# Ends of four program blocks, and the turning of an expert's 16 context rows, in a hybrid diffusion layer

## The reference, cut to what matters

```python
def _expert_choice_ffn(h, p):
    B, N, D = h.shape
    cap = EC_FACTOR * N // N_EXPERTS            # 256 latent rows, 16 context rows
    probs = jax.nn.softmax((h @ p['w_router']).astype(jnp.float32), axis=-1)
    gates, idx = lax.top_k(jnp.swapaxes(probs, 1, 2), cap)
    xsel = jax.vmap(lambda hb, ib: hb[ib])(h, idx)
    hid = jax.nn.silu(jnp.einsum('becd,edf->becf', xsel, p['w_gate'])) * jnp.einsum('becd,edf->becf', xsel, p['w_up'])
    yo = jnp.einsum('becf,efd->becd', hid, p['w_down']) * gates[..., None].astype(h.dtype)
    return jax.vmap(lambda ib, yb: jnp.zeros((N, D), yb.dtype).at[ib.reshape(-1)].add(yb.reshape(-1, D)))(idx, yo)

def _layer(x, cvec, p, states, grid):
    mods = (jax.nn.silu(cvec) @ p['w_ada'] + p['b_ada'])[..., None, :]
    sh1, sc1, g1, sh2, sc2, g2 = jnp.split(mods, 6, axis=-1)
    h = _rmsnorm(x, p['norm1_g']) * (1 + sc1) + sh1
    o, new_states = _mixers(h, p, states, grid)     # h @ w_in, three mixers, @ w_out
    x = x + g1 * o
    h = _rmsnorm(x, p['norm2_g']) * (1 + sc2) + sh2
    return x + g2 * _expert_choice_ffn(h, p), new_states
```

## Time and profile before

| | us |
|---|---|
| runs | 3442.53, 3443.15, 3450.62 |
| median | 3443.15 |
| profiled execution | 3448.97 |
| its span | 3447.2 |
| PE busy in the span | 3111.8 (90%) |
| VectorE, ScalarE, GpSimd busy | 2279.6, 1609.5, 878.8 |

### The profile page before, as it was taken

One profiled execution on the slowest core, in us unless ns is written; L12 is line 12 of the kernel. 1 busy time (PEld: TensorE's weight loads), 2 busy tenths in 40 slices (PEclk: granted clock), 3 DMA queues, 4 the chain that ended last, 5 costly groups with the idle time before them and its releaser, 6 DMA issues. The chain is left out here.

```text
span 3447.2 us, 90906 instructions
## 1 busy us (share of the span) xinstructions
PE 3111.8 (90%) x37105; PEld 2856.9 (83%) x37105; DVE 2279.6 (66%) x4490; ACT 1609.5 (47%) x2917; POOL 878.8 (25%) x1232
## 2 busy tenths in 40 slices
PE   7899989999689999999869961999999999999996
PEld 4887867767489999999857740999999999999996
DVE  5565549995478888888777758555555555555555
ACT  3313656665445545554456530444444444444454
POOL 0110000000066667676422201012111111111113
PEclk8999989999899999999989975999999999999998
DMA  6455336665644554444276632556656556556685
GB/s 203 139 163 170 94 88 203 201 198 152 186 122 108 131 151 111 110 109 109 56 209 186 177 125 76 165 186 196 208 186 195 186 185 194 185 184 190 206 286 187
DMA packets 583428, 561.43 MB, mean 163 GB/s; under 512 B 211550, under 2 KB 527262, under 8 KB 582138
## 3 DMA queue, kind: packets, MB, share of 16 engines
q1 hardware_dynamic: 546652, 446.02, 43.2%
q0 software_dynamic: 36016, 109.52, 10.8%
q10 hardware_dynamic: 432, 1.25, 0.1%
HBM read 418.33 MB, written 138.33 MB: 161 GB/s over the span
## 5 line engine op out<-in xcount | busy, mean ns | idle before, releaser
L3456 DVE TENSOR_TENSOR exp_wlo<-exp_raw,exp_whi 128x2048 fp32r<-128x2048 f32 x192 | 439.9, 2292 | 366.3 <-ACT exp_whi L3357 354.4
L3357 ACT CAST exp_whi<-exp_raw 128x2048 fp32r<-128x2048 f32 x189 | 360.0, 1905 | 76.8 <-DMA exp_raw<-in_w_up 74.2
L1042 PE MATMUL mix_acc<-proj_hThi,mix_wlo 128*128 128x448 f32 (+3 forms) x920 | 357.6, 389 | 14.4 <-DVE mix_wlo L1410 14.4
L1042 PE MATMUL mix_acc<-proj_hTlo,mix_whi 128*128 128x448 f32 (+3 forms) x920 | 335.6, 365 | 0.0
L1042 PE MATMUL mix_acc<-proj_hThi,mix_whi 128*128 128x448 f32 (+3 forms) x920 | 335.4, 365 | 0.0
L3286 PE MATMUL moe_o<-moe_hidhi,exp_wlo 128*128 128x272 f32 x1024 | 307.5, 300 | 2.6 <-DVE moe_hidlo L3570 2.6
L3286 PE MATMUL moe_g<-moe_xThi,exp_wlo 128*128 128x272 f32 x1024 | 300.1, 293 | 1.0 <-DVE moe_xTlo L3460 1.0
L3286 PE MATMUL moe_o<-moe_hidhi,exp_whi 128*128 128x272 f32 x1024 | 297.8, 291 | 0.0
L3286 PE MATMUL moe_g<-moe_xThi,exp_whi 128*128 128x272 f32 x1024 | 297.3, 290 | 0.0
L3286 PE MATMUL moe_u<-moe_xThi,exp_wlo 128*128 128x272 f32 x1024 | 296.7, 290 | 0.0
L3286 PE MATMUL moe_u<-moe_xThi,exp_whi 128*128 128x272 f32 x1024 | 296.4, 289 | 0.0
(11 more groups left out here) (395 smaller groups left out, 8539.5 us busy)
## 6 DMA issues: line engine op xcount, KB each, us to landing
exp_raw<-in_w_gate SPq DMA_DIRECT2D x64, 1024.0 KB, 5.0
exp_raw<-in_w_up SPq DMA_DIRECT2D x64, 1024.0 KB, 5.1
exp_raw<-in_w_down SPq DMA_DIRECT2D x64, 1024.0 KB, 6.7
scn_plain<-rec SPq DMA_DIRECT2D x68, 384.0 KB, 3.8
rec<-mix_arena SPq DMA_DIRECT2D x24, 896.0 KB, 4.4
proj<-mix_out POOLq DMA_DIRECT2D x88, 224.0 KB, 2.5
scn_grc<-grec SPq DMA_DIRECT2D x136, 128.0 KB, 3.9
mix_arena<-in_w_ada SPq DMA_DIRECT2D x12, 1024.0 KB, 5.8
```

The lines of the kernel that those rows point to most:

```text
L1042: mm = pe.matmul(acc[n % ACCS][0:width, 0:tn], wt[:, k, 0:width], hT[hp][:, k, t0:t0 + tn], start=k == 0 and i == 0, stop=k == KD - 1 and ...
L3357: act.copy(w[k % RING][0][:, :, :], raw[k % RAW][:, :, :]).then_inc(hi_done[k % RING], 1)
L3456: dve.tensor_tensor(w[k % RING][1][:, :, :], raw[k % RAW][:, :, :], w[k % RING][0][:, :, :], ALU.subtract).then_inc(lo_done[k % RING], 1)
```

## The change

Five edits. (a) Norm: GpSimd's wait for its stores is made by SP. (b) Mix: the last four of the 115 unit stores are issued by SP, in its slots ahead of the GLA record of that slot, with semaphores of their own; GpSimd's final waits are SP's. (c) Route: GpSimd has no list any more; the four picks stand first in the experts block. (d) Experts: the waits for the last scatters and stores are SP's. (e) `turn`: the third transposition takes 16 rows by 128 columns, with a 16 by 16 identity, and writes 16 columns.

```diff
@@ project_norm
+                for u in range(2):
+                    sp.wait_ge(v_stored[u], 32 * (9 - u))
...
-                for u in range(2):
-                    pool.wait_ge(v_stored[u], 32 * (9 - u))
@@ project_and_prepare
+    LAST_UNITS = UNITS - 4
...
+                def store_unit(n):
+                    c0, width = MIX_COLS[n // NB]
+                    t0, tn = MIX_BLOCKS[n % NB]
+                    sp.wait_ge(evacuated, n + 1)
+                    sp.dma_start(proj[c0:c0 + width, t0:t0 + tn], out[n % OUTS][0:width, 0:tn]).then_inc(last_stored[n % OUTS], 16)
+
                 for n in range(SLOTS):
+                    if LAST_UNITS < n <= UNITS:
+                        store_unit(n - 1)
...
                 sp.wait_ge(qk_stored, 16 * 4)
+                for u in range(OUTS):
+                    sp.wait_ge(out_stored[u], 16 * ((LAST_UNITS - 1 - u) // OUTS + 1))
+                    sp.wait_ge(last_stored[u], 16 * 2)
...
-                for n in range(SLOTS):
-                    if 1 <= n <= UNITS:
-                        store(n - 1)
-                for u in range(OUTS):
-                    pool.wait_ge(out_stored[u], 16 * ((UNITS - 1 - u) // OUTS + 1))
+                for n in range(LAST_UNITS):
+                    store(n)
...
-                    if n >= OUTS:
+                    if n >= LAST_UNITS + OUTS:
+                        act.wait_ge(last_stored[n % OUTS], 16)
+                    elif n >= OUTS:
                         act.wait_ge(out_stored[n % OUTS], 16 * (n // OUTS))
@@ stage_route
-            @block.gpsimd
-            def _(pool):
-                pool.wait_ge(out_done, 6)
-                pool.wait_ge(picked_out, 16)
-                for e in range(2):
-                    pick(pool, parts, picked, e)
+                sp.wait_ge(picked_out, 16)
@@ stage_experts
+                for u in range(HELD):
+                    sp.wait_ge(f_stored[u], 16 * held(u))
+                sp.wait_ge(late1_out, 48)
+                sp.wait_ge(late2_out, 48)
...
+                for e in range(2):
+                    pick(pool, parts, picked, e)
                 pool.memset(xs[:, 2, :], 0.0).then_inc(empty_zero, 1)
...
-                pool.wait_ge(late2_out, 48)
...
-                    for b in range(len(blocks)):
-                        mm = pe.transpose(ps_g[k % 2][:, b * P:(b + 1) * P], xs[:, b, k * P:(k + 1) * P], ident[:, :])
+                    for b, (s0, n) in enumerate(blocks):
+                        mm = pe.transpose(ps_g[k % 2][:, b * P:b * P + n], xs[0:n, b, k * P:(k + 1) * P], ident[0:n, 0:n])
```

More of the change, by code:

```diff
@@ L571, in project_and_prepare @@
             "raw_in", "high", "low", "product", "evacuated", "consts", "const_in"))
-        out_stored = [st.sem(f"out_stored{u}") for u in range(OUTS)]
+        out_stored, last_stored = ([st.sem(f"{x}_stored{u}") for u in range(OUTS)] for x in ("out", "last"))
         cvec_in, silu_done, picks, mod_part, mod_mm, mod_done = (st.sem(n) for n in (
```

## The result

The changed kernel takes 3463.43 us (median of 6 runs, 3459.57 to 3466.83), the kernel before 3442.84 (6 runs beside it, 3435.97 to 3450.62). The ratio is 1.0058, with a 95% interval of 1.0044 to 1.0071: slower by some 20 us, where 16 were forecast. The profiled executions, 3466.83 and 3448.97, differ by 17.9.

What follows compares the result with a forecast made beforehand. PE, busy throughout the experts, was taken to bound the kernel there. Block ends -10.6, turns +26.1 and first expert +0.6 gave +16.1 us on the median 3443.15, so 3459.3 us; range 3438 to 3469.

Steps and rivals of the forecast that it cites:

- Turns (e): Experts' turns: row steps around the 16-row transposition cost +26.1 us over 15 experts, +0.6 for the first expert.
- The first rival: Experts' turns: row steps cost nothing and the turns gain, so the kernel gets faster, 3427.5 us; chance 0.12.
- the second: Experts' turns: only the emptying is paid, the next weight load is hidden; +10.3 us, total 3443; chance 0.14.
- Mix (b): Mix block's end: GpSimd's drain runs beside the last units and the end hangs on SP; -6.4 us.
- the range for a hidden issue: Mix block's end: -5.5 us if a second store's issue is in the way, -6.9 if the issue is hidden.
- Norm (a): Norm block's end: GpSimd's drain starts earlier once SP waits for the stores; -1.0 us, between -1.9 and -0.2.
- end (d): Program's end after the experts: GpSimd's drain starts earlier beside the last scatter; -1.2 us, between -2.1 and -0.2.
- The open question: Block ends: whether GpSimd's drain can run while its transfers are under way or begins only with the last landing.
- A: Block ends: GpSimd's drain runs while its transfers are under way; -1.9 us in norm, -2.1 at the program's end.
- Picks (c): Route's end into experts: the drain of 6.70 us leaves route, picks run beside VectorE's splits; -2 us.
- The bound of +0.6: Route into experts: slow limit for moving the picks, +0.6 us, against -6.7 with nothing in the way.
- The third rival: Block ends give little: norm and end drains await the last landing, picks wait behind splits and loads; 3464.6 us, chance 0.16.

## Why the prediction came out

The direction, the size and the main term were right: 3459.3 was forecast, with 3438 to 3469 as the range. By its steps:

- **Turns (e), +26.1 and +0.6.** Measured 25.7, and 8.3 us instead of 8.1 from first turn to first product for the first expert. The price was read from rows of another stage and held: 0.202 and 0.250 us for a turn, where 0.205 and 0.255 had been worked out. Its parts are there too, though the records cut them elsewhere: the uncovered load lies inside the matmul that it is for. So the third transposition starts 0.201 after the second (0.108 + 0.093 of emptying), not 0.26 as the prediction's sign had it, the next 0.160 later (0.06 load, 0.01 stream, 0.09 emptying), and the one after that 0.166 later instead of 0.108 (the load of the step out). "Emptying" is the prediction's name for the 0.09 in which nothing starts; the traces show the gap and not what PE does in it. The Trainium skill's rule ("TensorEngine Tiling (Array Packing)", section "Key Properties") that a change of mode drains TensorE agrees with the 0.093 for rows. For columns the traces agree in part: behind the 16-column tile of a transposition back the products keep their pace, but in the scans a step of columns alone, from tiles of 64 rows by 64 columns to 64 by 128, shows the gap: 0.148 to 0.150 us at all 68 such steps of the kernel before, where pairs of equal tiles start 0.058 apart (one of them stands below the list). Why one change of columns costs 0.09 and the other nothing is open. The first rival (the steps cost nothing) and the second (0.086 for a turn, the next load unseen) are out.
- **Mix (b), -6.4.** From SP's drain to the end of the second barrier it was 930.0 to 938.4, and is 926.6 to 928.0: -7.0, and 1.4 us in all ten kernels with the edit. The +0.5 for SP's unit store ahead of record 7 is not there: from the issue of the last q/k record (L907, now L908) to SP's drain it takes 14.25 us without the edit and 14.28 to 14.31 with it, and the store ahead of record 6 cost nothing either, as assumed. SP came to its drain 0.5 us later in its stage, but that was so at the q/k record already and goes from -3.5 to +1.9 in the other kernels. So the edit is worth -6.9, the end of the range for a hidden issue. The length of GpSimd's drain was mis-sized, 14.3 us and not 9.1, and with 18 us to spare this cost nothing.
- **Norm (a), -1.0, and end (d), -1.2.** From the end of the last store's issue to the end of the barrier norm took 5.99 us and takes 4.41 to 4.42 in all ten kernels with the edit: -1.6. The last scatter to the end of the program is -2.2 in the same ten. The open question is answered for A: the drain runs beside transfers under way. At the end it needs 5.5 us from the last issue and not from the last landing, two us later. In norm it ends 3.2 us after the last issue, where it took 2.84 with all transfers landed, so nearly all of the -1.9 of A came.
- **Picks (c), -2: wrong.** It is +2.1 to the first turn (107.6 against 105.5; 106.7 to 107.2 in the four other kernels that move the picks and leave the splits alone, 105.1 to 105.5 in the four with all picks in route). The failing step is the end of picks, memset and gathers, put near 2148.1, 12.9 us after the barrier; they ended 16.2 after it. By this step alone the gain was -1.3 (2148.1 against 2149.4); the -2 was a choice between the bounds. The picks themselves were priced well (8.1 us from the first one's start to the last one's end, against 7.85). Left out were the 0.75 us until the first pick starts, 1.22 us in which the first gather waits for the picks' landing, which now lies on the path, and the fourth split, which now falls beside the first gather (2.74 us, not 1.0). PE's first turn comes 20.7 us after GpSimd's first instruction of the block, not 18. The bound of +0.6 was too narrow for the same reason. The third rival was right on this point and wrong on norm and the end, where A holds. The direction did not change, since 4 us stood against 25.

The step of columns in the scans (kernel before, PE alone):

```profile
960.30 0.22 PE L2058 MATMUL scn_b<-scn_U,scn_Ys 64*64 64x64 f32 x2
960.45 0.33 PE L2099 MATMUL scn_b<-scn_plain 64*128 64x64 f32 x2
```

The measured terms add up to -1.6 - 6.9 + 2.1 - 2.2 + 25.7 + 0.2 = +17.3, against 17.9 between the profiled executions; that these agree so well is partly luck. Between these two executions stages that the change doesn't touch differ by -2.2 (modulation), +2.1 (scans) and +1.8 (output); from the first expert's first product to the last product it is +23.5, less than the turns' 25.7; and the last scatter is issued 0.7 later behind the last product. The forecast of +16.1 came out by errors that cancel too: the picks lost 4 us more than forecast, the other ends gained 2.1 more, and the turns cost 0.8 less.

## What to carry to other kernels

Where PE is never idle, count a matmul's steps before its columns: here one transposition of 16 or 64 rows between full ones opened two gaps of 0.09 us and uncovered two weight loads, a net 0.2 us a turn for a tenth of a us of columns saved. Fill the rows instead (eight groups of 16 in one transposition) or leave the padding. A wait that is moved off GpSimd paid at the three ends where its drain was last (1.6, 6.9 and 2.2 us); work that is moved past a barrier must be priced with what runs beside it there and with the landing that it puts on the path.

## What the runs showed of the hardware

- With all its transfers landed, GpSimd's drain took about 0.082 us for each direct DMA that it had issued in the block: 2.84 us for 34 and 9.45 for 115, 6.99 for 85 at the end of the output block (L2542). An indirect one still to be handled adds about 1.3 us. The drain runs beside transfers and other engines' work, but the count then no longer gives its length: 13.8 to 14.3 us for the 111 stores of the changed mix block. Why is open.
- An indirect DMA that GpSimd issues beside VectorE's split takes 1.8 to 2.9 us and ends 0.74 to 0.93 us behind the split, without it 0.87 to 1.06; GpSimd's memset beside a split takes 0.95 as ever.
- In the six kernels with the picks moved, the last scatter is issued 19.0 us after the last product, in the four others with the same turn layout 18.3 to 18.4. Why the moved picks should cost 0.6 us at the far end is open; no run tried it.
- The scans, which no kernel here changes, took between 781.8 and 795.5 us from one profiled execution to the next; edits of a few us were therefore read from their own stage and not from the whole time.
